# Moving one 128x2048 operand sum from DVE to GpSimd at five operand changes of the feed-forward

## The reference

```
h = rmsnorm(x, g_mlp[l])
x = x + jnp.square(jax.nn.relu(h @ w_up[l])) @ w_down[l]
```

## Time and profile before

| what | value |
|---|---|
| median of 3 runs | 3044.73 us |
| profiled execution, and its span | 3040.73 us, 3038.9 us |
| mean granted TensorE clock in it | 0.967 of full speed |
| busy: PE, DVE, ACT, POOL | 92%, 63%, 45%, 31% |
| feed-forward, blocks 0 to 63 | from about 1780 us to the end |
| H sums T1 of the five later changes | 5 instructions of DVE, 2.28 us each |

### The profile page before, as it was taken

One profiled execution on the slowest core, in us unless ns is written; L12 is line 12 of the kernel. 1 busy time (PEld: TensorE's weight loads), 2 busy tenths in 40 slices (PEclk: granted clock), 3 DMA queues, 4 the chain that ended last, 5 costly groups with the idle time before them and its releaser, 6 DMA issues. The chain is left out here.

```text
span 3038.9 us, 43234 instructions
## 1 busy us (share of the span) xinstructions
PE 2804.4 (92%) x14883; PEld 2369.6 (78%) x14883; DVE 1911.2 (63%) x2799; ACT 1358.8 (45%) x2268; POOL 940.8 (31%) x747
## 2 busy tenths in 40 slices
PE   6999966879999997996899789999999999999999
PEld 5888853769889896885788668887888787878777
DVE  5334338758778786544667475657555868686864
ACT  4222224657667675222344355556555523242321
POOL 0111001745555552310000023333333344454443
PEclk9999988989999998997999989999999999999999
DMA  5332345273322203434132324333544375757555
GB/s 169 89 94 72 97 124 71 62 203 75 78 57 57 60 8 101 132 117 159 48 105 104 104 80 139 115 111 99 193 138 138 118 169 98 162 104 154 117 111 89
DMA packets 296148, 328.22 MB, mean 108 GB/s; under 512 B 114728, under 2 KB 221232, under 8 KB 295728
## 3 DMA queue, kind: packets, MB, share of 16 engines
q1 hardware_dynamic: 277568, 292.75, 32.6%
q0 software_dynamic: 18432, 33.56, 8.3%
HBM read 206.58 MB, written 126.89 MB: 110 GB/s over the span
## 5 line engine op out<-in xcount | busy, mean ns | idle before, releaser
L3124 PE MATMUL f_ps_bank<-f_big,h_wv 128*128 128x512 f32 x1792 | 704.9, 393 | 39.5 <-DVE f_big L2959 17.2
L3126 PE MATMUL f_ps_bank<-f_big,h_wv 128*128 128x512 f32 x1792 | 700.4, 391 | 0.0
L3125 PE MATMUL f_ps_bank<-f_big,h_wv 128*128 128x512 f32 x1792 | 700.4, 391 | 0.0
L3124 PEld LDWEIGHTS f_ps_bank<-f_big,h_wv 128*128 128x128 f32 x1792 | 338.4, 189 | 120.6 <-issue 31.1
L3126 PEld LDWEIGHTS f_ps_bank<-f_big,h_wv 128*128 128x128 f32 x1792 | 338.1, 189 | 71.1
L3125 PEld LDWEIGHTS f_ps_bank<-f_big,h_wv 128*128 128x128 f32 x1792 | 338.7, 189 | 69.6
L701 POOL TENSOR_TENSOR a_w<-a_on,a_left 128x640 f32<-128x640 f32 (+5 forms) x192 | 282.2, 1470 | 244.8 <-DVE a_left L751 115.5
L2955 DVE TENSOR_TENSOR h_wv<-h_w_raw,h_wv 128x512 fp32r<-128x512 f32 x189 | 238.6, 1263 | 156.5 <-ACT h_wv L2853 153.2
L2794 POOL TENSOR_TENSOR h_w_sum<-h_w_raw 128x512 f32<-128x512 f32 x63 | 89.8, 1425 | 730.4 <-DMA h_w_raw<-in_w_up 461.8
L2853 ACT ACTIVATE h_wv<-h_w_sum 128x512 fp32r<-128x512 f32 x252 | 159.0, 631 | 350.3 <-PE f_ps_bank L3126 347.5
L841 PE MATMUL a_ps_y<-a_wt,a_v 128*96 128x128 f32 x2176 | 269.5, 273 | 3.0 <-DVE a_yt L774 3.0
(11 more groups left out here) (387 smaller groups left out, 5584.3 us busy)
## 6 DMA issues: line engine op xcount, KB each, us to landing
h_w_raw<-in_w_up SPq DMA_DIRECT2D x32, 1024.0 KB, 6.8
a<-h_xr SPq DMA_DIRECT2D x128, 256.0 KB, 3.4
h_w_raw<-a SPq DMA_DIRECT2D x32, 1024.0 KB, 5.1
out<-h_xr POOLq DMA_DIRECT2D x128, 256.0 KB, 4.1
h_h_raw<-in_w_down SPq DMA_DIRECT2D x32, 512.0 KB, 6.6
p_xt<-in_x SPq DMA_DIRECT2D x16, 512.0 KB, 4.6
p_raw<-in_w_in SPq DMA_DIRECT2D x16, 512.0 KB, 5.5
q<-p_raw SPq DMA_DIRECT2D x64, 128.0 KB, 2.5
```

What stands on the lines that cost most here:

```text
L3124: pe.matmul(o, wv(i, 0)[:, k, :], hv(i, 0)[:, k, :], start=(k == 0), stop=False)
L3125: pe.matmul(o, wv(i, 0)[:, k, :], hv(i, 1)[:, k, :], start=False, stop=False)
L3126: mm = pe.matmul(o, wv(i, 1)[:, k, :], hv(i, 0)[:, k, :], start=False, stop=(k == KH - 1))
```

## The change

GpSimd gets a `sum_five_h` of its own, called after `sum_four(b)` for each block b of BOUNDS that its loop meets (16, 32, 40, 48, 56; the loop begins at 1), ahead of the C11 transfer. DVE keeps only the one of block 0. The new one waits for all three earlier H sums (3 in place of 2), and for TWO's low part as before.

```diff
+            def sum_five_h(chunk):
+                pool.wait_ge(h_summed[chunk], 3)
+                pool.wait_ge(hv_low, LOWS[chunk][TWO])
+                pool.tensor_tensor(T1[chunk], H22, T2[chunk], ALU.subtract).then_inc(h_summed[chunk], 1)
...
                 if b < END:
                     sum_four(b)
+                if b in BOUNDS:
+                    sum_five_h(BOUNDS.index(b))
                 if ALL <= b - 1 < END:
                     grow_out(b - 1, C11, 0, 0, 0)
...
-            def sum_five_h(chunk):
-                dve.wait_ge(h_summed[chunk], 2)
-                dve.wait_ge(hv_low, LOWS[chunk][TWO if chunk else SEVEN])
-                dve.tensor_tensor(T1[chunk], H22, T2[chunk], ALU.subtract).then_inc(h_summed[chunk], 1)
+            def sum_five_h():
+                dve.wait_ge(h_summed[0], 2)
+                dve.wait_ge(hv_low, LOWS[0][SEVEN])
+                dve.tensor_tensor(T1[0], H22, T2[0], ALU.subtract).then_inc(h_summed[0], 1)
...
-            sum_five_h(0)
+            sum_five_h()
...
-                        if (b, slot) == (first - 1, 3):
-                            sum_five_h(c)
...
-                if not plain and b == BLOCKS - 1:
-                    sum_five_h(1)
```

## The result

Ten runs of the changed kernel have a median of 3051.36 us (3047.99 to 3053.39), ten of the kernel before 3044.02 us (3040.99 to 3047.15). The ratio is 1.0027, with a 95% interval of 1.0018 to 1.0035: 7.3 us slower, between 5.5 and 10.7 us. The forecast was 3055, with a range of 3049 to 3060 and 0.78 on slower.

A forecast was written before the change was run, and what follows sets the result against it. TensorE bounds the kernel as a whole, but DVE's order of work bounds each change. 4 x 1.7 us for blocks 32 to 56 plus 3.8 at block 16 made 10.6 us on 3044.7, so 3055 us, range 3049 to 3060.

The forecast's parts named there:

- DVE's chain binds the four changes: Blocks 32, 40, 48, 56: TensorE waits on DVE's order of work, in which T1 takes 2.28 us.
- The sum shuts DVE out for its whole length: T1 on GpSimd: DVE operations with both inputs in SBUF stand until the sum ends, 4.56 us.
- the slope from 512 to 1024 columns: T1's time on GpSimd from lines 1756 and 1758: 1.096 us per further 512 columns, 4.59 us for 2048.
- line 701's: Other estimate of T1's time on GpSimd, from 896 and 1024 columns: 3.82 us, judged another operand layout's.
- 1.7 us at each of four: Blocks 32, 40, 48, 56: DVE free after 5.11 us instead of 3.40, so 1.7 us lost each, 6.8 together.
- the one wait at the start of block 32: DVE's wait for a store made from C12 shifts with the delay and swallows none of the 1.7 us.
- DVE has no idle time of its own in it: DVE's chain from block 31 into the next block: nothing there could swallow the 1.7 us delay.
- 3.8 us at block 16: Change at block 16: PE's FIVE starts some 3.8 us later; bounds 1.8 and 4.1 us.
- the way by ScalarE: Block 16: C12 comes 4.0 us later, and ScalarE carries the delay to the high part of FIVE.
- PE's waits should grow by about 10 us: Feed-forward: test that calls the prediction wrong if TensorE's waits don't grow by about 10 us.
- DVE goes on beside the sum: Rival: exclusion doesn't last a long GpSimd sum, so 9.3 us faster, 3035 us; chance 0.06.
- it loses the port twice: Rival: DVE's low parts of SEVEN's or FOUR's weights also lose to GpSimd, 16.0 us slower, 3061 us; chance 0.08.

The follow-up runs named there:

- E1: Kernel before, with T1 of the five later changes made by no engine, DVE only counting the semaphore; 3034.28 us against 3043.51, ratio 0.9967.
- E3: Changed kernel, with GpSimd making only the first 1024 of T1's 2048 columns; feed-forward 1257.4 us against 1266.4.
- E8: Changed kernel, with GpSimd copying H22 into T1 (one input) in place of the sum; feed-forward 1255.1 us against 1266.4.
- E6: Kernel before, with the change made only for blocks 32, 40, 48 and 56; 3047.30 us, ratio 1.0014.
- before, again: Kernel before, unchanged, profiled a second time; feed-forward 1261.4 us against 1257.1 in its first execution.
- E5: Kernel before, with the change made only for block 16; 3047.63 us against 3043.23, ratio 1.0012.
- the repeat: Changed kernel, with no further edit, profiled a second time; feed-forward 1268.5 us against 1266.4 in its first execution.
- E2: Changed kernel, with GpSimd writing zeros over T1 three times in place of the sum; feed-forward 1248.3 us against 1266.4.

## Why the prediction was right, and what was off

- **DVE's chain binds the four changes.** Right: E1 wins 9.2 us in the runs, where the same reasoning gave 9.
- **The sum shuts DVE out for its whole length.** Right, at a hold nearly twice the longest in the trace before. Estimate 4.56 us, measured 4.60 where nothing preceded it; the slope from 512 to 1024 columns was the right one, not line 701's. E3 and E8 show that the cost follows the hold.
- **1.7 us at each of four.** Right for three, too large for one. The DVE chain moved by 1.62 us in block 31 and the steps at 40, 48 and 56 are 1.5 to 1.7. At 32 the execution shows 1.0, and 0.9 up to block 36: "the one wait at the start of block 32 is for a store made from C12 and shifts with it" held (that `low_w` is dispatched 1.6 us later), but the `low_w` behind the wait took 1.65 us before, against GpSimd's sums, and 0.69 after, so 0.96 us came back. I had not looked at what stood behind the wait. The size repeats: E6, with the same code there, has 0.8 up to block 36, and the rest of its 1.8 is block 38's meeting, as most of the +1.8 of before, again, is.
- **Why 40 and 48 kept their 1.6 us.** Here the agreement owes something to luck. The low part of ONE's weights in blocks 40 and 48 got 1.3 us back too, 1.99 and 2.01 us before and 0.68 after. But DVE then waited 0.95 and 0.86 us for ScalarE's high part of FOUR, where it had waited for nothing before:

```profile
2565.90 1.99 DVE L2955 TENSOR_TENSOR h_wv<-h_w_raw,h_wv 128x512 fp32r<-128x512 f32 x1 [0.16 <-ACT h_wv L2853]
```

```profile
2571.63 2.29 DVE L2966 TENSOR_TENSOR f_big<-f_ps_th,f_big 128x2048 fp32r<-128x2048 f32 x1 [0.95 <-ACT f_big L2871]
```

  ScalarE's work there starts from C12, which DVE makes 1.6 to 1.7 us later, so the delay came round by ScalarE. The prediction's "DVE has no idle time of its own in it" was read in block 31 alone; at block 56 DVE waited 1.08 us for ScalarE already before.
- **3.8 us at block 16.** Right in size: 3.6, 3.7 in E5, 5.5 in the repeat, where 25 matmuls in place of 13 ran at half pace. The trace bears out the way by ScalarE: in block 16 DVE waited 1.09 and 1.11 us for it ahead of the low parts of FOUR and FIVE, which came 4.0 and 3.8 us later than before, counted from the start of block 15. No experiment took this way apart.
- **The sum.** 9.3 us in the first pair of executions, 7.1 in the second, 7.3 in the runs, 10.6 forecast. The term that was too large is that of block 32, by 0.7 us; the four others together fell 0.6 us short. The base is part of it: the profiled execution from which the steps were measured was a lucky one, 4.3 us shorter in the feed-forward than the next.
- **What would prove it wrong.** I wrote that PE's waits should grow by about 10 us. Counted in both from the wait before the last product of block 0, they grew from 29.4 to 34.0 us, by 4.6, so by its own words the prediction would have failed this test. It was badly chosen, since the text itself had a stretch at half pace hidden ahead of the next wait: the matmuls that start 0.40 to 0.46 us after the one before rose from 21 to 55, by 34 x 0.2 = 6.8 us. Matmuls slightly late, 0.25 to 0.34 us apart, became fewer and gave 2.0 us back. 4.6 + 6.8 - 2.0 = 9.4 us, and the feed-forward grew by 9.3. The 3.5 to 4.8 us waits for U4 at the four were as said (3.7 to 4.7 us).
- **The rivals.** That DVE goes on beside the sum is excluded (4.50 us for the `low_w` of FOUR). That it loses the port twice didn't occur at T1; it does occur elsewhere, as the second execution of before shows.

## What to carry to other kernels

Moving an elementwise sum from DVE to GpSimd pays only if DVE, while it runs, has operations that read PSUM or nothing to do: otherwise the move replaces DVE's 2.2 us by GpSimd's 4.6 us less what DVE can do beside it. Work out which of DVE's next operations read two SBUF operands before moving anything, cut a GpSimd sum in pieces if it must stand beside them, and look first for an idle stretch of DVE itself, as before block 33. And count TensorE's waits and its slow stretches together: here 5 to 12 matmuls ran at half pace behind each of the four waits of 3.7 to 4.7 us, and so part of the loss looks like work. Last, find out which meetings differ between two executions of the same kernel before a step of 1 us is put down to an edit.

## What was not expected of the hardware

- A fill of SBUF by GpSimd, 1.82 us for 128x2048 float32, runs beside DVE subtractions with no loss to either (E2), and a one-input copy of the same size takes 1.90 us and does hold them (E8). The copy costs two fifths of the sum's 4.60 us.
- Who goes first can be decided by a few hundredths of a us and be worth 2.3 us: the same program's `low_w` took 0.69 us in one execution and 4.17 in another. With the meeting in block 38 this makes single profiled executions of one kernel differ by 4 us in the feed-forward.
- How long a stretch at half pace follows a wait changes too: behind the wait of 3.7 to 3.9 us before FIVE of block 16 it was 6 matmuls in the kernel before and in E2, and 13 in E1 and E8.
